# Sums by one-pass products, differences on two engines: a chunk loop of a fused two-layer step

## The chip, the cores and the metric

One core of a Trainium2 chip runs the whole program. The metric is the device time of one execution in microseconds. Engines: TensorE (PE), with its weight loads in rows of their own (PEld), VectorE (DVE), ScalarE (ACT), GpSimd (POOL) and SyncE (SP), which here issues DMAs.

## The reference, cut to what matters

Two layers of a streaming encoder, for 512 prompt and 32 sample positions, f32. Layer 0 mixes by spatial gating and by a Mamba-2 scan. The two parts that the change touches:

```python
s = jnp.einsum('gij,bcjgd->bcigd', w, vc) + b_s[:, :n].T[None, None, :, :, None]   # gMLP, 8 groups, 128 positions
y = u * s
# SSD scan, 16 heads, within a chunk:
cs = jnp.cumsum(dt * a, axis=2)
seg = cs[:, :, :, None] - cs[:, :, None, :]
lmat = jnp.exp(jnp.where(tril, seg, -jnp.inf))
cb = jnp.einsum('bctgn,bcsgn->bctsg', cc, bc)          # 2 groups of 8 heads
y_diag = jnp.einsum('bctsg,bctsgr,bcsgrp->bctgrp', cb, lmat, xs)
# + contribution of the state before the chunk, and the state's update
```

The kernel takes chunks of 128 positions for the scan.

## The kernel before, in words

All activations lie as features on partitions, positions along the free dimension (512 prompt + 32 sample columns). Every dense layer is a row of "slabs" (`slab`, L298): 8 weight tiles of 128x128 against 544 columns, each in three one-pass products (fp32r) of a high and a low part, `w_hi*op_hi + w_hi*op_lo + w_lo*op_hi`, in two column halves of 256 and 288. SP loads the weights into a ring of four, ScalarE makes `w_hi` (L340), POOL `w_lo` (L414), four slabs ahead. All engines have hand-written instruction streams, coupled by counting semaphores; each engine goes through its stream in order.

Around the change:
- `spatial(g)` (L1001), after slabs 4 to 7 of phase `u` and 0 to 3 of `xbc`: per chunk of a group an f32 product that adds the bias (a table of ones times a row padded with zeros) and an f32 product with the spatial weights, into one PSUM bank. VectorE's `ya_out` reads it.
- `cs_sums` (L1017), once, after `spatial(0)`: cumulated sums `cs` and totals, from `da` (positions on partitions). VectorE's `dt_sums` (L1500) copies them out, then `spatial(1)` may run.
- The chunk loop: `chunk(p, rows)` on every engine, five passes: p = 0 the sample (32 rows), p = 1 to 4 the prompt's chunks (128 rows). In each PE turns x, B and C (L1073, L1078) and makes the score table; ScalarE copies them from PSUM (three copies, `x_copied`). Then for four blocks b of four heads `rows_of_cs(b)` (L1083) puts the chunk's sums of each head on all rows, one f32 product per head, in bank 3 (even b) or 2 (odd b); `segments(b)` (L1596, VectorE, L1606) subtracts the own row's sum and takes the minimum with the table `neg` (0 or -3e38), ScalarE's Exp follows, `mixed(b)` (L1610, VectorE, L1616) multiplies by the score table, and `diagonal(b)` (L1096) multiplies with `xs`. Two buffers (`mix`, two halves of 512) serve four blocks. Blocks 2 and 3 need the banks and buffers of 0 and 1 again. After that come the state's part, the state's update and the turn back (L1133).
- `between(n)` (L1053) fills PE's waits: n pieces of the phase `outa`, each an eighth of a slab (six one-pass products). `SSD_PIECES` says how many stand in each of five places. `SSD_MIXED` and `SSD_END` say where the ring's work for finished slabs goes on ScalarE, POOL and VectorE.
- POOL in a pass: `y_skip` (L560, D times x) as soon as the third copy is there, then `xsd` (L566).

```python
rows_of_cs(0); rows_of_cs(1); between(SSD_PIECES[p][0])
rows_of_cs(2); rows_of_cs(3); between(SSD_PIECES[p][1])
diagonal(0); diagonal(1); between(SSD_PIECES[p][2])
diagonal(2); diagonal(3)
```

Of the kernel before, what the change touches and what calls it, by code (L numbers as in the profile page):

```python
# [115 lines left out]
def build(nc, A, O):  # L116
# [27 lines left out]
    with ctx:  # L144
# [30 lines left out]
        neg = sb("neg", P)  # L175
# [255 lines left out]
        SSD_PIECES = ((1, 1, 5, 2, 2),) * NC + ((1, 1, 5, 2, 3),)  # L431
# [5 lines left out]
        N_CONSTS = 7  # L437

# [14 lines left out]
        def _(sp):  # L453
# [37 lines left out]
            for dst, name in ((tri, "tri"), (neg, "neg"), (head_rows, "head_rows"), (conv_state, "conv_state"),  # L491
                              (ffn_state, "ffn_state")):
                load(dst[:, :], A[name])
# [38 lines left out]
        def _(pool):  # L532
# [19 lines left out]

            def chunk(p, rows):
# [10 lines left out]
                if p:  # L564
# [55 lines left out]
        def _(act):  # L620
# [62 lines left out]
            for n in range(KD):  # L683
# [5 lines left out]
                if n == 1:  # L689
# [7 lines left out]
                    run(p_b, p_a, ACT.Exp, "dt_exp", scale=-1.0)  # L697
                if n == 5:
# [42 lines left out]
            def chunk(p, rows):  # L741
# [181 lines left out]
        def _(pe):  # L923
# [77 lines left out]
            def spatial(g):  # L1001
# [15 lines left out]
            def cs_sums():  # L1017
# [3 lines left out]
                mm(Q[:, 2, 128 + NC * SH:128 + NP_], ones[0:TS, :], da[0:TS, NC * SH:NP_]).then_inc(sem("cs_mm"), 1)  # L1021

            for n in range(KD):
# [13 lines left out]
                if n == U_FIRST:  # L1037
                    pe.wait_ge(sem("gm_mask"), 1)
# [834 lines left out]
```

## Time and profile before

| | |
|---|---|
| time, 3 runs | 1857.77 us median (1857.4 to 1858.76) |
| the profiled execution | 1858.24 us, its span 1856.5 us |
| PE busy | 1816.7 us (98%), 14145 matmul records |
| PEld busy | 1768.9 us (95%) |
| DVE, ACT, POOL busy | 955.9 (51%), 622.5 (34%), 847.5 (46%) us |
| mean granted PE clock | 0.991 of full speed |
| chain that ended last | PE 90%, DVE 6%, ACT 2% |

An f32 matmul of the program shows as two records, a one-pass (fp32r) one as a single record. A matmul's length in a row holds its way through the array too: matmuls overlap, so the pace is the distance from start to start. A row of the timeline merges neighbours of one line and form (x16 is 16 records), its length is from the first start to the last end. "[0.19 <- DVE ...]" is idle time of the engine before the row, and what ended it. PEclk is the clock granted to PE, 1.00 for 2.4 GHz and 0.50 for 1.2 GHz.

### The profile page before, as it was taken

Reading aid. Unit: us, or ns where it says so; the run is one execution under the profiler, and the core shown is the slowest. Engines: PE = TensorE matmul, PEld = TensorE weight load, DVE = VectorE, ACT = ScalarE, POOL = GpSimd, SP = SyncE. Lnnn points to the kernel's source line nnn. Section 1 sums busy time; section 2 is a strip of 40 time slices with the busy share of each in tenths; the row PEclk is TensorE's granted clock in tenths of the full one; section 3 lists DMA queues with packets and bytes.
Section 4 is the critical chain, followed back from the end, with each engine's and each line's share of the span. In section 5 each row is a group of like instructions: output and inputs, shape, how many; then the busy total and the mean of one; then the engine's idle time right before and its main releaser. Section 6 shows DMA issues by size and latency. Waiting matters only on the chain.

```text
span 1856.5 us, 34451 instructions
## 1 busy us (share of the span) xinstructions
PE 1816.7 (98%) x14145; PEld 1768.9 (95%) x14145; DVE 955.9 (51%) x1547; ACT 622.5 (34%) x896; POOL 847.5 (46%) x415
## 2 busy tenths in 40 slices
PE   8999999999999999999899999999999999999996
PEld 7999988999999999999899999999899999999995
DVE  6456777565533542556644441344555415515554
ACT  5334423343221222244433332233334313212342
POOL 4333423466544544565533334333365545544662
PEclk9999999999999999999999999999999999999998
DMA  6222201222342232223222222222122222222221
GB/s 231 79 73 69 80 23 35 74 86 80 114 138 89 81 103 90 74 79 98 80 77 77 77 76 80 88 77 78 54 91 82 89 90 90 91 92 82 66 93 48
DMA packets 49475, 156.80 MB, mean 84 GB/s; under 512 B 5984, under 2 KB 10208, under 8 KB 49376
## 3 DMA queue, kind: packets, MB, share of 16 engines
q1 hardware_dynamic: 43776, 147.67, 24.4%
q10 hardware_dynamic: 5600, 7.74, 1.3%
q8 instruction: 71, 1.16, 0.3%
q14 instruction: 28, 0.23, 0.0%
HBM read 149.75 MB, written 5.63 MB: 84 GB/s over the span
## 4 chain that ended last, share of the span: by engine, by line
PE 90%; DVE 6%; ACT 2%; issue 1%; POOL 0%; DMA 0%; DVEq 0%; POOLq 0%; ACTq 0%
PE proj L318 81%; PE Q L925 6%; DVE arena L1753 1%; ACT arena L622 1%; DVE op_lo L389 1%; DVE arena L1616 0%; DVE arena L1606 0%; ACT op_hi L376 0%; PE Q L1202 0%; DVE rstd L369 0%; DVE x L1755 0%; DVE ssq L1426 0%; PE proj L925 0%; DVE arena L1393 0%; PE Q L329 0%
## 5 line engine op out<-in xcount | busy, mean ns | idle before, releaser
L414 POOL TENSOR_TENSOR w_lo<-w_raw,w_hi 128x1024 fp32r<-128x1024 f32 (+2 forms) x276 | 652.3, 2364 | 760.0 <-ACT w_hi L340 759.7
L318 PE MATMUL proj<-op_hi,w_hi 128*128 128x256 f32 (+1 forms) x4272 | 895.6, 291 | 9.5 <-DVE op_lo L389 5.7
L318 PE MATMUL proj<-op_hi,w_lo 128*128 128x256 f32 (+1 forms) x4272 | 884.6, 288 | 0.0
L318 PE MATMUL proj<-op_lo,w_hi 128*128 128x256 f32 (+1 forms) x4272 | 877.8, 287 | 0.0
L318 PEld LDWEIGHTS proj<-op_hi,w_hi 128*128 128x128 f32 x4272 | 683.5, 189 | 22.6 <-issue 12.3
L318 PEld LDWEIGHTS proj<-op_lo,w_hi 128*128 128x128 f32 x4272 | 686.3, 189 | 0.0
L318 PEld LDWEIGHTS proj<-op_hi,w_lo 128*128 128x128 f32 x4272 | 682.0, 188 | 0.0
L340 ACT ACTIVATE w_hi<-w_raw 128x1024 fp32r<-128x1024 f32 (+2 forms) x276 | 284.8, 1032 | 651.0 <-PE proj L318 650.0
L1393 DVE TENSOR_TENSOR arena<-proj,rstd 128x512 f32<-128x512 f32 (+1 forms) x143 | 98.7, 690 | 220.9 <-PE proj L318 195.4
L1400 DVE TENSOR_TENSOR x<-proj,x 128x512 f32<-128x512 f32 x72 | 49.7, 690 | 223.2 <-PE proj L318 223.2
L622 ACT ACTIVATE arena<-arena 128x32 f32<-128x32 f32 (+5 forms) x217 | 106.0, 514 | 54.6 <-DVE arena L1606 33.2
L604 POOL TENSOR_TENSOR arena<-arena,rstd 128x544 f32<-128x544 f32 x44 | 60.0, 1363 | 140.6 <-ACT arena L622 140.6
L405 POOL TENSOR_TENSOR ssq<-ssq,sq 128x544 f32<-128x544 f32 x56 | 90.3, 1613 | 67.7 <-ACT sq L384 67.7
L925 PE MATMUL Q<-arena 128*128 128x256 f32 (+9 forms) x524 | 104.7, 344 | 1.3 <-DVE arena L1616 0.8
L1709 DVE SCALAR_TENSOR_TENSOR arena<-arena,vec 128x546 f32<-128x546 f32 x88 | 96.4, 1095 | 12.4 <-DVE arena L1709 0.3
L925 PEld LDWEIGHTS Q<-arena 128*128 128x128 f32 (+3 forms) x524 | 71.9, 178 | 25.6 <-issue 16.2
L1717 DVE TENSOR_TENSOR arena<-proj,arena 128x512 f32<-128x512 f32 x44 | 30.4, 692 | 120.0 <-POOL arena L604 120.0
L389 DVE SCALAR_TENSOR_TENSOR op_lo<-x,vec,op_hi 128x544 fp32r<-128x544 f32 x48 | 72.1, 1514 | 37.0 <-ACT op_hi L376 33.5
L1707 DVE TENSOR_SCALAR arena<-arena,vec 128x546 f32<-128x546 f32 x44 | 78.2, 1777 | 8.3 <-DVE arena L1697 8.3
L622 ACT ACTIVATE ffn_tail<-arena 128x4 f32 (+1 forms) x44 | 9.1, 206 | 200.0 <-DVE arena L1709 200.0
L1720 DVE TENSOR_TENSOR op_lo<-arena,op_hi 128x544 f32 (+1 forms) x44 | 47.5, 1080 | 40.3 <-ACT op_hi L622 40.3
L622 ACT ACTIVATE op_hi<-arena 128x544 f32 (+2 forms) x46 | 31.0, 678 | 67.5 <-DVE arena L1718 67.5
(171 smaller groups left out, 1040.2 us busy)
## 6 DMA issues: line engine op xcount, KB each, us to landing
w_raw<-in_w_gu SPq DMA_DIRECT2D x88, 512.0 KB, 3.4
w_raw<-in_w_down SPq DMA_DIRECT2D x32, 512.0 KB, 3.4
w_raw<-in_w_heads_a SPq DMA_DIRECT2D x30, 512.0 KB, 3.4
w_raw<-in_w_heads_b SPq DMA_DIRECT2D x18, 512.0 KB, 3.4
w_raw<-in_w_gate SPq DMA_DIRECT2D x16, 512.0 KB, 3.4
w_raw<-in_w_xbc SPq DMA_DIRECT2D x12, 512.0 KB, 3.3
w_raw<-in_w_down SPq DMA_DIRECT2D x16, 384.0 KB, 3.0
w_raw<-in_w_v SPq DMA_DIRECT2D x8, 512.0 KB, 8.2
```

Of the source, the lines that this page charges most:

```text
L318: last = nc.tensor.matmul(proj[:, 2 * g.mod(2) + half, 0:size], w[:, lo:lo + P], o[:, at:at + size], start=(k == 0 and j == 0), stop=(k == ...
L340: nc.scalar.activation(w_hi[:, c:c + width], w_raw[:, c:c + width], ACT.Copy).then_inc(w_hi_done, 1)
L389: nc.vector.scalar_tensor_tensor(out=part(op_lo[ops], n, 0, T), in0=src, scalar=col(gain, n), in1=part(op_hi[ops], n, 0, T), op0=ALU.mult, ...
L405: nc.gpsimd.tensor_tensor(ssq[:, :], ssq[:, :], sq[:, q * T:(q + 1) * T], ALU.add)\
L414: nc.gpsimd.tensor_tensor(w_lo[:, c:c + width], w_raw[:, c:c + width], w_hi[:, c:c + width], ALU.subtract).then_inc(w_lo_done, 1)
L604: nc.gpsimd.tensor_tensor(fsgr[:, q * T:(q + 1) * T], fsg[:, q * T:(q + 1) * T], rstd[:, :], mul).then_inc(sem("f_scaled"), 1)
L622: ins = nc.scalar.activation(dst, src, f, **kw)
L925: return nc.tensor.matmul(out, w, o, start=start, stop=stop)
L1393: a = tt(two(dst(0, TP)), out_prompt(g, rows), two(by[0:rows, f_at:f_at + TP]), mul)
L1400: tt(two(part(x, n, 0, TP)), out_prompt(g), two(part(x, n, 0, TP)), add)
L1707: ins = nc.vector.tensor_scalar(acc, src, w, col(f"fb{layer}", t + -layer * FT), mul, add)
L1709: ins = stt(out=acc, in0=src, scalar=w, in1=acc, op0=mul, op1=add)
```

## The change

- Bias: `bs_pad` holds the bias in rows 0 and 32. ScalarE makes `bias_r` (fp32r) of it, VectorE replaces rows 32 to 63 by the remainder. Each spatial group gets its bias by two one-pass products of 256 columns (two chunks each) and one of 32, where it had four f32 products of 128 and one of 32.
- Sums: `cs_sums` also makes the cumulated sums with heads on partitions (48 rows: three times 16), five more f32 products. ScalarE rounds them into `cs_t` (fp32r), VectorE puts the remainder in rows 32 to 47. `spatial(1)` waits for that.
- POOL's `by_block(p)` spreads a chunk's sums into `cs_b`, four copies each masked by `pick`, so that products with a column of `pick_r` as weights give the rows of four heads. It runs one pass ahead, behind `xsd`; the first one stands before the loop, behind the ring's work for slab `outa` 0.
- `rows_of_cs(b)` is two one-pass products of 256 columns (64 in the sample's pass) in place of four f32 products.
- The differences of blocks 0 and 2 are four Relu on ScalarE (from PSUM, own sum as bias), those of blocks 1 and 3 four tensor_scalar on VectorE. `neg` is gone; the mask is a product of the score table with `tri`, once per pass on VectorE, after `xs`.
- `SSD_PIECES` of the prompt's passes: 1, 2, 4, 2, 2 for 1, 1, 5, 2, 2 (the last with 3).
- The `memset` of `s_prompt` moves from the middle of phase `u` to its end.

The diff, cut:

```diff
+cs_t = nc.alloc_sbuf_tensor_at("cs_t", [P, T], R, offset=ssq_at)
+cs_b = nc.alloc_sbuf_tensor_at("cs_b", [P, 2 * 512], R, offset=sq_at)
+ones_r = nc.alloc_sbuf_tensor_at("ones_r", [P, P], R, offset=w_dt_at)
...
+bias_r = nc.alloc_sbuf_tensor_at("bias_r", [P, D], R, offset=arena_at + 4 * r.at)
 gain_rows = r.take(D)
+da_3 = arena[:, r.at:r.at + 3 * NP_]
...
-SSD_PIECES = ((1, 1, 5, 2, 2),) * NC + ((1, 1, 5, 2, 3),)
+SSD_PIECES = ((1, 1, 5, 2, 2),) + ((1, 2, 4, 2, 2),) * (NC - 1) + ((1, 2, 4, 2, 3),)
...
+def by_block(p, rows):
+
+    c = NC if p == 0 else p - 1
+    if p >= 2:
+        pool.wait_ge(sem("cs_rows"), 4 * (p - 1))
+    out = cs_b[0:HL, (p % 2) * 512:(p % 2) * 512 + 4 * rows].rearrange("p (j t) -> p j t", j=4)
+    nc.gpsimd.tensor_tensor(out, cs_t[0:HL, c * CH:c * CH + rows].unsqueeze(1).broadcast_to([HL, 4, rows]),
+                            pick[0:HL, 0:4].unsqueeze(2).broadcast_to([HL, 4, rows]), mul)\
+        .then_inc(sem("by_block"), 1)
+
+pool.wait_ge(sem("cs_split"), 1)
+pool.wait_ge(consts_in, 16 * N_CONSTS)
+pool.wait_ge(sem("gm_lo"), GROUPS)
+by_block(0, TS)
...
+    if p < NC:
+        by_block(p + 1, CH)
...
+    if n == 0:
+        act.wait_ge(sem("gm_in"), 32)
+        act.wait_ge(sem("v_gained"), GROUPS)
+        run(bias_r[0:64, :], bs_pad[0:64, :], ACT.Copy, "bias_hi")
+        act.wait_ge(sem("wdt_lo"), 1)
+        act.wait_ge(consts_in, 16 * N_CONSTS)
+        run(ones_r[0:64, :], ones[0:64, :], ACT.Copy, "ones_set")
+        run(pick_r[0:HL, :], pick[0:HL, 4:8], ACT.Copy, "ones_set")
+    if n == U_FIRST:
+        act.wait_ge(sem("cs_mm"), 1)
+        act.wait_ge(sem("gm_vn"), GROUPS)
+        run(cs_t[0:HL, 0:TP], Q[0:HL, 3, :], ACT.Copy, "cs_hi")
+        act.wait_ge(sem("cs_copied"), 1)
+        run(cs_t[0:HL, TP:T], Q[0:HL, 2, 256:256 + TS], ACT.Copy, "cs_hi")
...
-        act.wait_ge(sem("seg_done"), 16 * p + 4 * b + 4)
         m = four(mix[0:rows, (b % 2) * 512:(b % 2 + 1) * 512])[:, :, 0:rows]
-        run(m, m, ACT.Exp, "decayed")
+        if b % 2 == 0:
+            act.wait_ge(sem("cs_rows"), 4 * p + b + 1)
+            if p or b:
+                act.wait_ge(sem("y_mm"), 4 * p + b - 1)
+            for j in range(4):
+                h = c * SH + 4 * b + j
+                ins = run(m[:, j, :], Q[0:rows, 3, j * rows:(j + 1) * rows], ACT.Relu,
+                          bias=cs[0:rows, h:h + 1], scale=-1.0)
+            ins.then_inc(sem("gaps_act"), 1)
+            act.wait_ge(sem("gaps_act"), 2 * p + b // 2 + 1)
+            run(m, m, ACT.Exp, "decayed", scale=-1.0)
+        else:
+            act.wait_ge(sem("gaps_dve"), 2 * p + b // 2 + 1)
+            run(m, m, ACT.Exp, "decayed")
...
-    bias = bs_pad[:, g * P:(g + 1) * P]
+    bias = bias_r[0:64, g * P:(g + 1) * P]
     for c in range(NC):
+        if c % 2 == 0:
+            mm(Q[:, q, c * CH:(c + 2) * CH], ones_r[0:64, :], bias.unsqueeze(1).broadcast_to([64, 2, P]),
+               stop=False)
         at = g * VT + c * P
-        mm(Q[:, q, c * CH:(c + 1) * CH], ones[:, :], bias, stop=False)
         mm(Q[:, q, c * CH:(c + 1) * CH], v_tok[:, at:at + P], w_spatial[:, g * P:(g + 1) * P], start=False,
-           stop=True)
-    mm(Q[:, q + 1, 0:TS], ones[:, :], bias[:, 0:TS], stop=False)
+           stop=(c % 2 == 1))
+    mm(Q[:, q + 1, 0:TS], ones_r[0:64, :], bias[:, 0:TS], stop=False)
     mm(Q[:, q + 1, 0:TS], v_tok[:, g * VT + TP:(g + 1) * VT], w_spatial[:, g * P:g * P + TS],
        start=False).then_inc(sem("gm_s"), 1)
...
-    mm(Q[:, 2, 128 + NC * SH:128 + NP_], ones[0:TS, :], da[0:TS, NC * SH:NP_]).then_inc(sem("cs_mm"), 1)
+    mm(Q[:, 2, 128 + NC * SH:128 + NP_], ones[0:TS, :], da[0:TS, NC * SH:NP_])
+    for c in range(NC + 1):
+        rows = CH if c < NC else TS
+        out = Q[0:HL, 3, c * CH:(c + 1) * CH] if c < NC else Q[0:HL, 2, 256:256 + TS]
+        last = mm(out, da_3[0:rows, c * HL:(c + 1) * HL], tri[0:rows, 0:rows])
+    last.then_inc(sem("cs_mm"), 1)
...
     if n == U_FIRST + 1:
-        pe.wait_ge(sem("cs_copied"), 1)
+        pe.wait_ge(sem("cs_split"), 1)
...
             pe.wait_ge(sem("x_copied"), 3 * p + 3)
-        elif b >= 2:
-            pe.wait_ge(sem("seg_done"), 16 * p + 4 * (b - 1))
-        bank = 3 - b % 2
-        for j in range(4):
-            h = hc + 4 * b + j
-            last = mm(Q[0:rows, bank, j * P:j * P + rows], da[0:rows, h:h + 1].broadcast_to([rows, rows]),
-                      tri[0:rows, 0:rows])
+        elif b == 2:
+            pe.wait_ge(sem("gaps_act"), 2 * p + 1)
+        elif b == 3:
+            pe.wait_ge(sem("gaps_dve"), 2 * p + 1)
+        if b == 0:
+            pe.wait_ge(sem("by_block"), p + 1)
+        at = (p % 2) * 512
+        for half in range(2):
+            cols = slice(half * 2 * rows, (half + 1) * 2 * rows)
+            last = mm(Q[0:rows, 3 - b % 2, cols], pick_r[0:HL, b:b + 1].broadcast_to([HL, rows]),
+                      cs_b[0:HL, at + cols.start:at + cols.stop])
         last.then_inc(sem("cs_rows"), 1)
...
-    pe.wait_ge(sem("seg_done"), 16 * p + 16)
+    pe.wait_ge(sem("gaps_act"), 2 * p + 2)
+    pe.wait_ge(sem("gaps_dve"), 2 * p + 2)
...
+    link(nc.vector.tensor_copy(da_3.rearrange("p (c r h) -> p c r h", r=3, h=SH),
+                               by_head(da).unsqueeze(2).broadcast_to([P, NC + 1, 3, SH])))
...
+    lo = slice(2 * SH, HL)
+    dve.wait_ge(sem("cs_hi"), 1)
+    tt(cs_t[lo, 0:TP], Q[lo, 3, :], cs_t[lo, 0:TP], sub)
+    dve.wait_ge(sem("cs_hi"), 2)
+    tt(cs_t[lo, TP:T], Q[lo, 2, 256:256 + TS], cs_t[lo, TP:T], sub).then_inc(sem("cs_split"), 1)
...
+        dve.wait_ge(sem("bias_hi"), 1)
+        tt(bias_r[32:64, :], bs_pad[32:64, :], bias_r[32:64, :], sub).then_inc(sem("bias_lo"), 1)
...
-        nc.vector.memset(s_prompt, 0.0).then_inc(sem("s_zero"), 1)
...
+nc.vector.memset(s_prompt, 0.0).then_inc(sem("s_zero"), 1)
...
+    dve.wait_ge(sem("x_copied"), 3 * p + 3)
+    cb = two(bc_tok[0:rows, 256:512])[:, :, 0:rows]
+    tt(cb, cb, tri[0:rows, 0:rows].unsqueeze(1).broadcast_to([rows, 2, rows]), mul)\
+        .then_inc(sem("cb_masked"), 1)
...
-        if b >= 2:
+        if p or b >= 2:
             dve.wait_ge(sem("y_mm"), 4 * p + b - 1)
-        elif p:
-            dve.wait_ge(sem("y_mm"), 4 * p - 1 + b)
         for j in range(4):
             h = c * SH + 4 * b + j
-            at = (b % 2) * 512 + j * P
-            stt(out=mix[0:rows, at:at + rows], in0=Q[0:rows, 3 - b % 2, j * P:j * P + rows],
-                scalar=cs[0:rows, h:h + 1], in1=neg[0:rows, 0:rows], op0=sub, op1=ALU.min)\
-                .then_inc(sem("seg_done"), 1)
+            at = 512 + j * P
+            ins = nc.vector.tensor_scalar(mix[0:rows, at:at + rows], Q[0:rows, 2, j * rows:(j + 1) * rows],
+                                          cs[0:rows, h:h + 1], 0.0, sub, ALU.min)
+        ins.then_inc(sem("gaps_dve"), 1)
...
-        dve.wait_ge(sem("x_copied"), 3 * p + 3)
+        dve.wait_ge(sem("cb_masked"), p + 1)
...
-    segments(0)
     segments(1)
     mixed(0)
     mixed(1)
-    segments(2)
     segments(3)
...
```

## Rows read from the trace of the kernel before

**Rows 1.** Windows, first pass (two) and third: span, length, busy PE/PEld/DVE/ACT/POOL, PEclk, DMA.

```profile
219.40:226.40 7.00, 4.18 (x51) 3.13 (x50) 4.88 (x13) 4.82 (x11) 4.85 (x2) 1.00 0.32 113
226.40:233.20 6.80, 6.80 (x42) 6.32 (x43) 4.30 (x12) 0.81 (x3) 2.25 (x2) 0.50 0.03 10
266.95:289.24 22.29, 21.98 (x163) 19.46 (x162) 16.52 (x34) 6.80 (x11) 6.55 (x3) 1.00 0.08 24
```

**Rows 2.** Timeline of PE in the third pass: start, length, instruction, idle before.

```profile
268.48 2.01 PE L925 MATMUL Q<-tri,arena 128*128 128x128 f32 x16
270.25 0.50 PE L318 MATMUL proj<-op_hi,w_hi 128*128 128x256 f32 x2
274.15 2.00 PE L925 MATMUL Q<-arena 128*128 128x64 f32 x16 [0.19 <-DVE arena L1616]
```

**Rows 3.** The timelines of VectorE, ScalarE and GpSimd there

```profile
268.70 1.23 DVE L1594 TENSOR_TENSOR arena<-arena 128x1024 f32<-128x1024 f32 x1 [1.77 <-ACT arena L622]
269.84 2.15 DVE L1606 SCALAR_TENSOR_TENSOR arena<-Q,arena,neg 128x128 f32<-128x128 f32 x8
271.91 2.78 DVE L1616 TENSOR_TENSOR arena<-arena 128x512 f32<-128x512 f32 x2
267.58 1.70 ACT L622 ACTIVATE arena<-Q 128x512 f32<-128x512 f32 x3 [1.29 <-PE Q L1073]
269.36 2.33 POOL L560 TENSOR_TENSOR arena<-arena,head_rows 128x1024 f32<-128x1024 f32 x1 [9.69 <-ACT arena L622]
271.65 1.90 POOL L566 TENSOR_TENSOR arena<-arena 128x1024 f32<-128x1024 f32 x1
```

**Rows 4.** The chain of waits there (start, length, what)

```profile
271.91 2.19 DVE arena L1616
```

**Rows 5.** The timeline of PE in the first spatial group

```profile
104.84 0.38 PE L925 MATMUL Q<-arena,ones 128*128 128x128 f32 x2
106.63 0.31 PE L925 MATMUL Q<-arena,ones 128*128 128x32 f32 x2
107.88 0.52 PE L318 MATMUL proj<-op_hi,w_hi 128*128 128x256 f32 x2
108.24 0.41 PE L318 MATMUL proj<-op_lo,w_hi 128*128 128x256 f32 x2
108.49 0.41 PE L318 MATMUL proj<-op_hi,w_lo 128*128 128x256 f32 x2
```

**Rows 6.** The chain of waits at the second spatial group

```profile
114.14 2.24 PE Q L925 x20
```

**Rows 7.** The timelines of VectorE and GpSimd in the u stage

```profile
107.93 2.41 DVE L1512 TENSOR_SCALAR v_tok<-v_tok,ssq 32x128 f32<-32x128 f32 x1
113.67 0.23 DVE L1504 TENSOR_TENSOR arena<-Q,arena 128x80 f32<-128x80 f32 x1
107.54 2.73 POOL L414 TENSOR_TENSOR w_lo<-w_raw,w_hi 128x1024 fp32r<-128x1024 f32 x1 [4.95 <-ACT w_hi L340]
```

**Rows 8.** Groups of ScalarE by form: busy us, mean ns, idle before.

```profile
L622 ACT ACTIVATE arena<-Q 128x128 f32<-128x128 f32 x2 | 0.5, 277 | 11.1 <-PE Q L1133 11.1
```

**Rows 9.** The timelines of PE, VectorE, ScalarE and GpSimd in the first pass

```profile
222.01 0.43 PE L925 MATMUL Q<-tri,arena 32*32 32x32 f32 x8
228.48 1.91 PE L925 MATMUL Q<-arena 32*32 32x64 f32 x16
222.55 2.43 DVE L1594 TENSOR_TENSOR arena<-arena 32x1024 f32<-32x1024 f32 x1 [1.92 <-ACT arena L622]
222.81 1.28 ACT L622 ACT_TABLE_LOAD   x1
221.55 2.36 POOL L414 TENSOR_TENSOR w_lo<-w_raw,w_hi 128x1024 fp32r<-128x1024 f32 x1 [4.14 <-ACT w_hi L340]
```

**Rows 10.** The timeline of PE at two long idles

```profile
903.37 0.82 PE L318 MATMUL proj<-op_hi,w_hi 128*128 128x256 f32 x2 [5.18 <-DVE op_lo L389]
1396.09 0.49 PE L318 MATMUL proj<-op_hi,w_hi 128*128 128x256 f32 x2 [1.39 <-issue]
```

More of the change, by code:

```diff
@@ L161, in build @@
         ARENA = 15200
+        arena_at = nc.sbuf_base
         arena = sb("arena", ARENA)
+        ssq_at = nc.sbuf_base
         ssq = sb("ssq", T)
@@ L174, in build @@
         tri = sb("tri", P)
-        neg = sb("neg", P)
+        sq_at = nc.sbuf_base
         sq = sb("sq", 2 * T)
@@ L184, in build @@
         conv_tail = sb("conv_tail", XBC * 6)
+        w_dt_at = nc.sbuf_base
         w_dt = sb("w_dt", 8 * SH)
@@ L187, in build @@
         w_dt_lo = sb("w_dt_lo", 8 * SH, R)
+        pick = sb("pick", 8)
+        pick_r = sb("pick_r", 4, R)
         rstd_root = sq[:, 0:T]
+        cs_t = nc.alloc_sbuf_tensor_at("cs_t", [P, T], R, offset=ssq_at)
+        cs_b = nc.alloc_sbuf_tensor_at("cs_b", [P, 2 * 512], R, offset=sq_at)
+        ones_r = nc.alloc_sbuf_tensor_at("ones_r", [P, P], R, offset=w_dt_at)
         class Region:
@@ L437, in build @@
         N_CONSTS = 7
+        HL = 3 * SH
         def heads(eng, head, between, drain=None):
@@ L490, in _ @@
             sp.dma_start(gain_rows, A["gain_rows"]).then_inc(sem("gain_in"), 16)
-            for dst, name in ((tri, "tri"), (neg, "neg"), (head_rows, "head_rows"), (conv_state, "conv_state"),
-                              (ffn_state, "ffn_state")):
+            for dst, name in ((tri, "tri"), (head_rows, "head_rows"), (conv_state, "conv_state"),
+                              (ffn_state, "ffn_state"), (pick, "pick")):
                 load(dst[:, :], A[name])
@@ L573, in _ @@
                     low_ahead(pool, PH["outa"], At(n))
+            pool.wait_ge(sem("by_block"), NC + 1)
             pool_squares(pool, "n_yb", "n_in")
@@ L1037, in _ @@
                 if n == U_FIRST:
+                    pe.wait_ge(sem("bias_lo"), 1)
+                    pe.wait_ge(sem("ones_set"), 2)
                     pe.wait_ge(sem("gm_mask"), 1)
@@ L1831 @@
     arrays["tri"] = (t[:, None] <= t[None, :]).astype(f32)
-    arrays["neg"] = np.where(t[:, None] <= t[None, :], 0.0, -3e38).astype(f32)
     kdec = np.exp(lg[None, :] * (CH - 1.0 - t)[:, None])
@@ L1851 @@
     arrays["w_spatial"] = a["gm_w_s"].transpose(2, 0, 1).reshape(P, -1)
-    arrays["bs_pad"] = np.concatenate([a["gm_b_s"].reshape(1, -1), np.zeros((P - 1, D), f32)])
+    arrays["bs_pad"] = np.zeros((P, D), f32)
+    arrays["bs_pad"][0] = arrays["bs_pad"][32] = a["gm_b_s"].reshape(-1)
+    row, four = np.arange(P)[:, None], np.arange(4)[None, :]
+    used = (row < SH) | ((row >= 2 * SH) & (row < 3 * SH))
+    arrays["pick"] = np.concatenate([used & (row % 4 == four), used & (row % SH // 4 == four)], 1).astype(f32)
     arrays["ssm_state"] = a["state_ssm"][0].reshape(SH * SP_, SN).T
```

## The prediction, made before the changed kernel was run

> **What bounds the kernel now.** I read the shares of busy time first: TensorE (PE) works 1816.7 of 1856.5 us, every other engine about half or less, so only work that leaves PE, or waits put in front of it, can move the end. The change touches two stages, so next come the stretches of the chunk loop [rows 1]: in the third of its five passes (266.95 to 289.24) PE is busy 21.98 of 22.29 us at full clock. Then that pass in order of time. PE [rows 2]: four heads' sums are four f32 products of 128 columns; 16 records from 268.48 to 270.25 are eight products, 0.221 us each. An eighth of a slab of `outa` follows (a piece, 0.75 us at the pace below), eight more products, another piece, and the diagonal products at 274.15 after 0.19 us idle for VectorE. So the pass is PE's own work end to end. The other engines [rows 3]: VectorE makes `xs` 268.70 to 269.93, the eight differences of L1606 straight behind it (0.26 us apart), then the products of L1616; ScalarE copies until 269.28; GpSimd (POOL) runs L560 and L566 from 269.36 to 273.55. One thing here decides my forecast: the first L1616 holds the chain for 2.19 us, from 271.91 to 274.09 [rows 4], though the two together take 2.78 [rows 3], which leaves the second about 0.65. It ran only when L566 was done, while L1606, which reads PSUM, passed beside L560 undisturbed.
>
> **Bias.** Per group the spatial stage issues eight f32 products of 128 columns between 104.84 and 106.63, 0.224 us each, then a bias product of 32 columns, 0.31 us with its tail, of which I take 0.14 as its own [rows 5]. Four plus the small one are bias: 4 x 0.224 + 0.14 = 1.04 us. After: two one-pass products of 256 columns. A one-pass pair of 256 + 288 columns takes 0.25 (108.24 to 108.49), so 256 columns take 0.118; the small one at most that. But a one-pass pair behind f32 products takes 0.36 (107.88 to 108.24), 0.11 more, and two of the three now stand behind f32: 0.118 + 0.228 + 0.17 = 0.52. Saved 0.52 a group, 4.2 us in eight. Bounds: 0.3 (each weight change costs more) to 0.85 (no extra), so 2.4 to 6.8. PE stands directly on the path here.
>
> **Sums.** `cs_sums` gets four f32 products of 128 columns and one of 32: 4 x 0.224 + 0.14 = +1.04 us (0.6 to 1.3, as 48 weight columns may load faster). The second spatial group now waits for `cs_split`, not `cs_copied`. The latter came with L1504, over at 113.90, and PE came at 114.14 [rows 6, 7]: 0.24 us of slack. The new chain adds a ScalarE copy, VectorE's two differences (512 and 32 columns) and a hop, about 0.85 us; VectorE comes earlier, for the `memset` of 1024 columns left this stretch and the smaller copy into `da_3` joined it (an estimated 0.55 net). I take 0 and keep up to 0.9. The bias split (some 1 us each on ScalarE and VectorE) ends long before its use at 104.84; the memset falls into a stretch where VectorE waits. The changed constants are one small DMA for another. Nothing for these.
>
> **Rows of sums.** Per prompt pass 16 products of 0.221 (3.54 us) become eight of 0.118 (0.94): 2.6 us less PE work, 10.4 in four passes. With no new wait the loop would give that.
>
> **What the loop waits for instead**, third pass, in the old clock:
> - `rows_of_cs(1)` waits for the third copy, 269.28, behind the first block's products. Those took 0.9 us and hid it; now they take 0.24 from 268.48. PE idles about 0.55. The piece then ends near 270.2.
> - `rows_of_cs(2)` waits for ScalarE's four Relu. Nearest row: a 128x128 copy from PSUM, 277 ns [rows 8]; at 0.2 to 0.28 each they end 270.1 to 270.4. Hidden.
> - `rows_of_cs(3)` waits for `gaps_dve`, VectorE's block 1. Before it in VectorE's queue stands the new mask product on the score table, with two SBUF inputs. L560 has been waiting since 269.36 and starts when `xs` ends, for 1.83 us, to 271.69. That POOL goes first where both wait is shown at 107.54 [rows 7]: its operation took 2.73 us where the same one takes 2.36 [rows 9], so it stood 0.37 behind the VectorE operation of that moment, and the next of VectorE (107.93, all SBUF, a 32x128 piece) took 2.41 and ended just after it. So the mask runs 271.69 to 271.97, the differences to 273.0. PE stands from about 270.3 to 273.05.
> - Two pieces (1.5 us) bring `diagonal(0)` to 274.7. The mask has pushed L566 to 271.97 to 273.85, so `mixed(0)` is 273.85 to 274.4. Behind L566 POOL now has `by_block(p+1)`, half of L566's elements, about 0.95 us (0.6 to 1.3), to 275.35. `mixed(1)` ends at 275.9, and `diagonal(1)`, ready at 275.6, starts 275.95 and is done at 277.05.
> Before, both diagonals ended at 276.15 (2.00 from 274.15) with two pieces behind them; now at 277.05 with three (0.75 more). Net 276.3: 0.15 us later than before, with all 2.6 spent. The later half changes little: Relu and differences of blocks 2 and 3 are done before the four remaining pieces end at 280. Passes two and four, where a weight operation of POOL comes first, come out alike, the last, without `by_block`, 0.4 earlier. Loop: about +0.2 us (bounds -2 to +3 for `by_block` and the mask).
>
> The difference on VectorE is now a tensor_scalar that reads PSUM. L1606 (PSUM) was not held, the tensor_scalar at 107.93 (all SBUF) was [rows 3, 7]; I take the first by its source. Held like the second it would wait behind L566 too, +1.9 us a pass, 7.6 in all.
> The Trainium skill ("SBUF — State Buffer", section "SBUF: two separate sides") says that VectorE and GpSimd share one port pair as an exclusive lock for a whole instruction, on VectorE's side for two SBUF inputs or a two-port mode. By that rule the tensor_scalar from PSUM is free and the mask is held; the trace agrees on the forms it has. By the rule the loop's sum is +0.2, by the nearest row of the same operation +7.8.
>
> **First pass.** `rows_of_cs(0)` ran at 222.01 [rows 9]. It now waits for `by_block(0)`, queued on POOL behind L414 (221.55 to 223.90), and there VectorE's waiting `xs` goes first, to 224.98. So it starts near 225.3; ScalarE's Relu end at 226.3; the table load (1.28), so far done during a wait, can only follow them, so Exp ends at 228.0, `mixed(0)` behind L566 at 229.3, `mixed(1)` behind `by_block(1)` at 230.45. The diagonals, begun at 228.48 and done at 230.4, end near 231.4: +1.0 us (0 to +3, for the clock here).
>
> **The clock.** It is at its low level from 226.4 to 233.2 after seven microseconds in which PE was busy 4.18 [rows 1]. A 5.18 us idle at 898.2 was followed by low clock, one of 1.39 at 1394.7 was not [rows 10]. The new idles are 2.7 to 3.0 us each, with 0.55 and 0.35 beside them: 3.7 of some 7 us, more than the 2.8 before the fall at 226.4, but with denser work around. A fall costs at most half of 6.8 us, 3.4, less what lies in a wait: I take 3.0. I expect two falls in the four prompt passes: +6.0 (0 to +12).
>
> **Sum**, against the profiled execution's own 1858.24 (span 1856.5): -4.2 + 1.04 + 0.2 + 1.0 + 6.0 = +4.0, 1862.3. The median of the runs lies 0.47 lower: 1861.8.
>
> **Rivals.**
> 1. The same waits, no fall of the clock in the four prompt passes. For: the single idle of 1.39 us was not followed by one [rows 10]. Against: the new one is twice that. -4.2 + 1.04 + 0.2 + 1.0 = -2.0: 1855.8.
> 2. The mask product isn't held (VectorE keeps the port from `xs` to the mask). Then the differences end 1.7 us earlier, PE idles 1.0 instead of 2.75, and of 2.6 us a pass about 1.7 stay: -6.8 for the loop, no fall: -4.2 + 1.04 - 6.8 + 1.0 = -9.0: 1848.8. Faster, and it decides wherever the differences end before about 271.5. Against: 107.54 [rows 7].
> 3. All four passes fall (+12) and the first pass stays low longer (+1): 1869. For: the 7 us comparison above.
> 4. The tensor_scalar is held too: another 7.6 on the forecast, 1869.4.
>
> **Chances.** Forecast with one to three falls, 1858.8 to 1864.8: 0.45. Rival 1: 0.18. Rival 2: 0.26. Rivals 3 and 4: 0.11. A change under 0.2% (3.7 us, about what can be told from none) is 1854.1 to 1861.5: it holds most of rival 1 (0.15) and the one-fall end of the forecast (0.15), 0.30. Slower: the rest of the forecast (0.30) and rivals 3 and 4, 0.41. Faster: rival 2, and rival 1 with the bias at its upper bound (0.03), 0.29. Range 1849 to 1869; the forecast's own is 1857 to 1866.
>
> **What would show it.** Spatial groups of about 1.6 us instead of 2.15. In the prompt passes one PE idle of 2.7 to 3 us before the fourth block of sums, released by VectorE's differences, and a mask product of about 2 us that ends just after L560. `mixed(1)` lengthened by `by_block`. In the first pass PE idle over 3 us, released by POOL. PEclk at 0.5 after some of the idles. Wrong if the mask takes 0.3 us or PE's idle stays under 1.2, and wrong in the clock part if PEclk stays at 1.0 through all four.

## The result, and the profile after

The changed kernel takes 1876.22 us (median of 4, 1872.8 to 1877.4) where the kernel before takes 1858.26 on the same chip: ratio 1.0094, 95% interval 1.0081 to 1.0107. It is slower by 18 us. The forecast was 1861.8, the range 1849 to 1869: wrong. The direction had a chance of 0.41.

The profiled execution took 1875.27 us (span 1873.5), 17.0 more than before's 1858.24. PE works 1824.1 us of it, 7 more, though it has 166 fewer matmul records. To find where they are lost, lay the starts of the five passes side by side: the first of the products that turn (transpose) x in each pass. The end is the same product behind the last turn back in each trace. All in us:

| | first turn at | pass 1 | 2 | 3 | 4 | 5 | end |
|---|---|---|---|---|---|---|---|
| before | 220.58 | 23.80 | 22.57 | 22.29 | 23.37 | 23.03 | 335.64 |
| changed | 223.76 | 22.91 | 27.12 | 23.89 | 27.65 | 27.64 | 352.98 |

So 3.2 us are lost ahead of the loop and 14.2 in it; 0.3 are won behind it. First the stretches of the loop in the changed kernel (the columns of [rows 1]; the last row stops 2.1 us short of its pass's end at 352.98):

```profile
223.76:246.68 22.92, 19.21 (x137) 14.77 (x138) 13.31 (x26) 7.68 (x21) 8.63 (x6) 0.93 0.07 24
246.68:273.80 27.12, 24.63 (x139) 21.35 (x137) 17.41 (x28) 8.54 (x18) 10.60 (x5) 0.81 0.12 39
273.80:297.69 23.89, 21.66 (x138) 18.39 (x137) 16.50 (x27) 8.98 (x19) 8.16 (x4) 0.93 0.07 23
297.69:325.34 27.65, 24.37 (x139) 21.09 (x137) 18.34 (x29) 9.04 (x19) 11.04 (x5) 0.81 0.12 39
325.34:350.90 25.56, 23.33 (x128) 20.06 (x127) 14.32 (x24) 7.73 (x17) 6.74 (x3) 0.80 0.07 21
```

Before, the third pass stood at a granted clock of 1.00 [rows 1]; now every pass has a stretch at 0.50 (1.2 GHz). In the trace's record of the clock these low stretches last 3.4, 10.2, 3.4, 10.2 and 10.2 us, one a pass, where before had one of 6.8 in the first.

What TensorE did before each fall, its timeline with the idle ahead of a row in brackets:

```profile
228.46 0.31 PE L980 MATMUL Q<-cs_b,pick_r 48*32 48x64 f32 x4 [3.19 <-POOL cs_b L570]
253.06 0.79 PE L980 MATMUL Q<-cs_b,pick_r 48*128 48x256 f32 x2 [2.12 <-DVE arena L1687]
276.19 0.50 PE L980 MATMUL Q<-cs_b,pick_r 48*128 48x256 f32 x2 [0.26 <-ACT arena L651]
279.91 0.79 PE L980 MATMUL Q<-cs_b,pick_r 48*128 48x256 f32 x2 [1.85 <-DVE arena L1687]
304.86 0.79 PE L980 MATMUL Q<-cs_b,pick_r 48*128 48x256 f32 x2 [2.91 <-DVE arena L1687]
331.45 0.79 PE L980 MATMUL Q<-cs_b,pick_r 48*128 48x256 f32 x2 [1.85 <-DVE arena L1687]
```

The four idles that VectorE's differences (L1687) end are the forecast one, ahead of the fourth block of sums; the low clock begins inside them or as they end (252.62, 279.92, 303.82, 331.12). Before, the only idle among the rows of the third pass was 0.19 us, ahead of the diagonal products [rows 2]. Why L1687 is late stands in the third pass's timelines of VectorE and GpSimd, which answer to [rows 3]:

```profile
275.55 1.23 DVE L1672 TENSOR_TENSOR arena<-arena 128x1024 f32<-128x1024 f32 x1 [1.76 <-ACT arena L651]
276.69 2.13 DVE L1676 TENSOR_TENSOR arena<-arena,tri 128x256 f32<-128x256 f32 x1
278.74 1.11 DVE L1687 TENSOR_SCALAR arena<-Q,arena 128x128 f32<-128x128 f32 x4
279.78 2.79 DVE L1697 TENSOR_TENSOR arena<-arena 128x512 f32<-128x512 f32 x2
276.21 2.33 POOL L586 TENSOR_TENSOR arena<-arena,head_rows 128x1024 f32<-128x1024 f32 x1 [9.69 <-ACT arena L651]
278.50 2.08 POOL L592 TENSOR_TENSOR arena<-arena 128x1024 f32<-128x1024 f32 x1
280.54 1.48 POOL L570 TENSOR_TENSOR cs_b<-cs_t,pick 48x512 fp32r<-48x512 f32 x1
```

The mask product (L1676) lasts 2.13 us and ends at 278.82, 0.28 behind GpSimd's L586 (278.54). Free of GpSimd it takes 0.42 (shown below). A row that is so much longer than the operation itself is called held here. L1687, from PSUM, passes beside L592 at full pace: four in 1.11 us. The two L1697 take 2.79 together, where two free ones take 1.48 (also below). In the chain of waits the mask is now on the path (in place of [rows 4]):

```profile
276.69 2.13 DVE arena L1676
```

Ahead of the loop, the second spatial group in the chain, then its timeline; [rows 6] had 2.24 us, [rows 5] the first group's parts:

```profile
115.24 2.45 PE Q L980 x13
```

```profile
115.17 0.38 PE L980 MATMUL Q<-bias_r,ones_r 64*128 64x256 f32 x1
115.48 0.71 PE L980 MATMUL Q<-arena,v_tok 128*128 128x128 f32 x4
116.12 0.38 PE L980 MATMUL Q<-bias_r,ones_r 64*128 64x256 f32 x1
```

With 13 records instead of 20 the group is longer. From a bias product to the next product pass 0.31 us, where the forecast had 0.12; and from the start of four records of 128 columns (two products, 0.45) to the next bias product 0.64. From the start of one group to the start of the next it is 8.55 us, before 8.24.

### The profile page after: what moved, and what is told of

It reads as the page before. It is cut to its first block, busy times and chain, and to the rows that moved or that the text cites. A ratio compares the mean times of both kernels' runs of the same rounds, so it can differ in the third digit from the quotient of the medians.

```text
span 1873.5 us, 34149 instructions
## 1 busy us (share of the span) xinstructions
PE 1824.1 (97%) x13979; PEld 1767.8 (94%) x13979; DVE 953.8 (51%) x1516; ACT 634.4 (34%) x941; POOL 856.2 (46%) x420
## 4 chain that ended last, share of the span: by engine, by line
PE 85%; DVE 6%; issue 5%; ACT 2%; POOL 2%; DMA 0%; POOLq 0%; DVEq 0%; ACTq 0%
PE proj L328 76%; PE Q L980 6%; POOL w_lo L424 1%; DVE arena L1832 1%; DVE op_lo L399 1%; ACT arena L651 1%; DVE arena L1676 0%; ACT op_hi L386 0%; DVE ssq L1495 0%; PE Q L1271 0%; DVE rstd L379 0%; DVE x L1834 0%; PE proj L980 0%; PE Q L339 0%; DVE arena L1462 0%
## 5 line engine op out<-in xcount | busy, mean ns | idle before, releaser
L424 POOL TENSOR_TENSOR w_lo<-w_raw,w_hi 128x1024 fp32r<-128x1024 f32 (+2 forms) x276 | 654.7, 2372 | 769.0 <-ACT w_hi L350 768.7
L328 PEld LDWEIGHTS proj<-op_hi,w_hi 128*128 128x128 f32 x4272 | 686.2, 189 | 24.5 <-issue 13.3
L980 PE MATMUL Q<-arena 128*128 128x256 f32 (+9 forms) x524 | 108.5, 354 | 1.0 <-DVE arena L1697 0.4
L980 PEld LDWEIGHTS Q<-arena 128*128 128x128 f32 (+3 forms) x524 | 76.2, 189 | 24.5 <-issue 16.2
```

Source lines behind the costliest of these rows:

```text
L328: last = nc.tensor.matmul(proj[:, 2 * g.mod(2) + half, 0:size], w[:, lo:lo + P], o[:, at:at + size], start=(k == 0 and j == 0), stop=(k == ...
L424: nc.gpsimd.tensor_tensor(w_lo[:, c:c + width], w_raw[:, c:c + width], w_hi[:, c:c + width], ALU.subtract).then_inc(w_lo_done, 1)
L980: return nc.tensor.matmul(out, w, o, start=start, stop=stop)
```

## The experiments

Times are medians; beside each stands the ratio to the kernel before on the same chip with its interval. The kernel before gave 1857.9 to 1858.1 throughout.

### Idle filled with products

```diff
                 rows_of_cs(2)
+                for _ in range((0, 16, 14, 22, 14)[p]):
+                    mm(Q[:, 1, 0:256], op_hi[1][:, 0:P], op_hi[1][:, 0:256])
                 rows_of_cs(3)
```

> The changed kernel, with 16, 14, 22 and 14 throwaway one-pass products of 256 columns on TensorE ahead of the fourth block of sums of the four prompt passes (about 0.11 us each, no more than the 1.9 to 2.9 us that TensorE stands idle there); they lengthen no wait. Theory A (the granted clock, which falls after these idles, costs most of the 18 us): the low stretches of 3.4 and 10.2 us go, 12 to 16 us faster than the changed kernel, about 1861 to 1864. Rival B (the waits themselves cost the time, the clock is a by-product): the same idle is only filled, 1875 to 1877.

1863.2 us, 13.0 less than the changed kernel (1.0024, 1.0014 to 1.0033). The windows of the second to fourth pass:

```profile
249.81:272.51 22.70, 22.30 (x154) 18.99 (x153) 17.32 (x28) 8.42 (x18) 10.61 (x5) 1.00 0.15 47
272.51:294.92 22.41, 22.04 (x152) 18.72 (x151) 16.50 (x27) 8.97 (x19) 8.16 (x4) 1.00 0.08 24
294.92:318.33 23.41, 22.95 (x160) 19.64 (x159) 18.32 (x28) 9.03 (x19) 11.03 (x5) 1.00 0.14 46
```

The products do nothing useful and shorten no wait: in the second pass the fourth block of sums starts 6.39 us behind the pass's start, in the changed kernel 6.38. Yet the four prompt passes take 91.6 us instead of 106.3: with the idle filled the clock stays at 2.4 GHz, and that is worth 14.7 us. What is left is what the kernel before takes there (91.3): the waits have eaten the saving of 2.6 us a pass and no more. The first pass, left as it was, had a low stretch of 13.7 us this time (26.0 us against 22.9), which takes 3.1 back. It does the same work after the same idle of 3.19 us in both, so the idle alone does not set how long the clock stays low.

### Bias products over 128 rows

```diff
-                bias = bias_r[0:64, g * P:(g + 1) * P]
+                bias = bias_r[:, g * P:(g + 1) * P]
```
(and `ones_r[:, :]` in both products; rows 64 to 127 of the bias are zero)

> The changed kernel, with the bias products of the spatial groups over 128 contraction rows (rows 64 to 127 hold zeros) instead of 64. Theory C (TensorE pays some 0.2 to 0.3 us each time it goes between a product over 64 rows and one over 128): a group falls from 2.45 us to 1.7 to 1.9, eight groups, 4 to 6 us faster than the changed kernel, about 1871. Rival D (going between one-pass and f32 products is what costs, whatever their rows): a group stays at 2.4, 1876.

1867.64 us, 8.6 less (1.0050, 1.0033 to 1.0067). The chain's row and the group's timeline:

```profile
115.17 1.65 PE Q L980 x13
```

```profile
115.17 0.38 PE L980 MATMUL Q<-bias_r,ones_r 128*128 128x256 f32 x1 [0.65 <-DVE cs_t L1580]
115.39 0.61 PE L980 MATMUL Q<-arena,v_tok 128*128 128x128 f32 x4
115.75 0.36 PE L980 MATMUL Q<-bias_r,ones_r 128*128 128x256 f32 x1
115.95 0.61 PE L980 MATMUL Q<-arena,v_tok 128*128 128x128 f32 x4
```

The same products over twice the rows are faster: group to group 7.46 us instead of 8.55. Call it a going when TensorE goes from a product over 128 rows to one over 64, or back. The three bias products of a group mean six goings, 1.09 / 6 = 0.18 us each.

### f32 bias products over 64 rows in the kernel before

```diff
-                bias = bs_pad[:, g * P:(g + 1) * P]
+                bias = bs_pad[0:64, g * P:(g + 1) * P]
```
(and `ones[0:64, :]`)

> The kernel before, with its f32 bias products of the spatial groups over 64 contraction rows instead of 128 (the left-out rows hold zeros); no one-pass product anywhere in them. Theory C, on its own: each of the five bias products of a group, which stand between products over 128 rows, costs some 0.3 us more, 1.5 us a group, eight groups: 8 to 13 us slower than before, 1866 to 1871. Rival D (rows cost nothing, one-pass beside f32 does): 1858.

1873.59 us, 15.7 slower than before (1.0088, 1.0071 to 1.0105), above the expected 8 to 13.

```profile
115.30 4.01 PE Q L925 x20
```

```profile
115.23 0.48 PE L925 MATMUL Q<-arena,ones 64*128 64x128 f32 x2
115.64 0.49 PE L925 MATMUL Q<-arena,v_tok 128*128 128x128 f32 x2
116.06 0.48 PE L925 MATMUL Q<-arena,ones 64*128 64x128 f32 x2
```

Group to group 10.08 instead of 8.24: 1.84 us for ten goings, 0.18 each again, with no one-pass product in it. So the change of rows is what costs, not one-pass beside f32. The expectation was low for two reasons: a bias product costs 0.37 us more (in and out), not 0.3, which makes 14.7 us in eight groups; and the first pass is 1.1 us longer (24.92 against 23.80), with a low stretch of 10.2 us instead of 6.8. The Trainium skill ("TensorEngine Tiling (Array Packing)", section "Key Properties") says that "Changing tiling mode (not just tile) drains the TensorE"; its section "Tiling Modes" lists 64 rows as a mode of their own. A drain at each going would fit the 0.18 us, but no trace here shows the mode or the drain; the price is from the traces.

### The bias part alone, over 128 rows, in the kernel before

The diff is the change's bias part with the two lines above.

> The kernel before, with the change's bias part alone, and its one-pass bias products over all 128 contraction rows (rows 64 to 127 hold zeros). Theory C (the going between 64 and 128 rows ate the gain of the bias part): a spatial group takes 1.65 us as in the run with 128 rows instead of 2.15 to 2.2, eight of them, 4 us faster than before, about 1854. Rival D (the bias part has no gain of its own, what the run with 128 rows won lay in the changed kernel's other parts): 1858.

1854.17 us (0.9977, 0.9967 to 0.9986): 3.9 faster than before, as expected. Over all 128 rows, the bias part alone is a gain of about the forecast size, though not by the forecast's sum: a group saves 0.78 us (8.24 to 7.46), 6.2 in eight; a new wait of 1.61 us for VectorE's `dt_sums` ahead of the second group and a first pass that is 1.1 longer (24.88 against 23.80, low stretch 10.2 us) take most of the difference back.

### Sums products over 128 rows

```diff
+            nc.gpsimd.tensor_scalar(cs_b[:, :], w_spatial[:, 0:1024], 0.0, None, mul)
-     pick_r[0:HL, b:b + 1].broadcast_to([HL, rows]), cs_b[0:HL, ...]
+     pick_r[:, b:b + 1].broadcast_to([P, rows]), cs_b[:, ...]
```

> The changed kernel, with the one-pass products of the sums over 128 contraction rows (rows 48 to 127 hold zeros, set once by GpSimd ahead of the loop) instead of 48. Theory C: about 0.3 us less of TensorE for each of four blocks of a pass; what of it is on the path is the first and the second block and what stands behind the third, 0.3 to 1.0 us a pass, 2 to 5 us in all. Rival D: nothing, 1876.

1868.69 us, 7.5 less (1.0065, 1.0048 to 1.0082), more than either theory gave. PE's idle ahead of the fourth block is not shorter (10.1 us in four passes, 8.7 in the changed kernel), but each low stretch of the prompt passes lasts 3.4 us where three lasted 10.2: passes of 24.0, 23.8, 24.7 and 24.5. What the rows do for the work itself is seen further down, where no idle disturbs it.

### The mask product behind the differences

```diff
+                segments(1)
                 dve.wait_ge(sem("x_copied"), 3 * p + 3)
                 tt(cb, cb, tri...)      # the mask product
-                segments(1)
                 mixed(0)
```

> The changed kernel, with VectorE's mask product behind the differences of the second block instead of ahead of them; nothing else is moved. Theory E (the mask is held until GpSimd's product ends, and it alone makes the fourth block of sums wait): the idle of 1.9 to 2.9 us there goes, the mask is held further behind by GpSimd's next product instead, the third and fourth head block's chain is 1 to 2 us earlier and fewer clock falls stay: 1862 to 1870. Rival F (the idle only goes to the first diagonal product, which waits for the masked table through the same chain, and the clock falls there): 1874 to 1877.

1865.94 us, 10.3 less (1.0040, 1.0027 to 1.0053). The idle ahead of the fourth block goes in three of the four prompt passes; in the second the diagonals wait instead, 1.12 and 0.34 us, for products held in their turn. VectorE there:

```profile
253.00 1.09 DVE L1697 TENSOR_TENSOR arena<-arena,tri 128x256 f32<-128x256 f32 x1
254.19 3.65 DVE L1692 TENSOR_TENSOR arena<-arena 128x512 f32<-128x512 f32 x2
```

In the fourth pass a shorter idle stays ahead of the fourth block, and the clock is low from 302.86 for 10.2 us (the pass takes 26.4):

```profile
301.91 0.50 PE L980 MATMUL Q<-cs_b,pick_r 48*128 48x256 f32 x2 [0.85 <-DVE arena L1682]
```

### GpSimd's products behind the second masked-decay product

```diff
                 pool.wait_ge(sem("x_copied"), 3 * p + 3)
+                pool.wait_ge(sem("mixed"), 4 * p + 2)
```

> The changed kernel, with GpSimd's three products of a pass (skip term, xsd, next sums table) let go only once VectorE has done its second masked-decay product of that pass. Theory E (VectorE and GpSimd hold one another off, and so the mask, the two products and with them the fourth block of sums come late): the mask takes 0.4 us instead of 2.1, the next two products 0.7 each, TensorE no longer stands idle ahead of the fourth block, the falls of the granted clock go with the idle; four passes of 27.1, 23.9, 27.6 and 25.3 us come to 22 to 23 each, 12 to 17 us faster than the changed kernel, 1859 to 1864. Rival G (it is ScalarE's four-step differences and the chain through them that is late): the idle stays, 1874 to 1877; or the three products come so late that the end of the pass waits for them, 1876 and more.

1858.96 us, 17.3 less (1.0000, 0.9990 to 1.0009): as much as the whole loss, with one wait. The ten runs lie between 1854.4 and 1860.1. VectorE in the third pass, then the passes' windows:

```profile
272.89 0.42 DVE L1677 TENSOR_TENSOR arena<-arena,tri 128x256 f32<-128x256 f32 x1
273.23 1.12 DVE L1688 TENSOR_SCALAR arena<-Q,arena 128x128 f32<-128x128 f32 x4
274.27 1.48 DVE L1698 TENSOR_TENSOR arena<-arena 128x512 f32<-128x512 f32 x2
```

```profile
249.03:270.00 20.97, 20.20 (x139) 17.01 (x137) 14.87 (x28) 8.42 (x18) 9.96 (x5) 1.00 0.15 51
270.00:290.66 20.66, 20.14 (x138) 16.95 (x137) 14.07 (x27) 8.97 (x19) 7.80 (x4) 1.00 0.09 26
```

The mask takes 0.42 us (2.13 when held). Of the 2.6 us of PE work saved in a pass, 1.6 now show (22.57 to 20.97, 22.29 to 20.66).

### The first sums table early

```diff
+            by_block(0, TS)
             low_ahead(pool, PH["outa"], At(0))
-            by_block(0, TS)
```

> The changed kernel, with GpSimd's first sums table ahead of its low split of the second outa slab instead of behind it. Theory H (TensorE's 3.2 us idle in the first pass is this product's queueing behind the split): that idle goes and the first pass is 2 to 3 us shorter, unless the clock falls otherwise: 1873 to 1875. Rival: the split comes 1.4 us later and the first piece of outa waits for it, 1876.

1877.02 us (1.0092, 1.0076 to 1.0109): no gain. The 3.2 us idle released by GpSimd is gone, and one of 3.3 us stands ahead of the fourth block of the same pass, since VectorE's mask is now held beside GpSimd's L586 (227.06 to 229.94):

```profile
225.75 2.43 DVE L1672 TENSOR_TENSOR arena<-arena 32x1024 f32<-32x1024 f32 x1 [1.95 <-ACT arena L651]
228.11 1.91 DVE L1676 TENSOR_TENSOR arena<-arena,tri 32x64 f32<-32x64 f32 x1
```

```profile
230.71 0.32 PE L980 MATMUL Q<-cs_b,pick_r 48*32 48x64 f32 x2 [3.30 <-DVE arena L1687]
```

The idle had a second cause behind the first. Both come from VectorE and GpSimd holding one another: in the changed kernel the first table stands behind L424 and VectorE's `xs`, here the mask behind L586.

### All four, and three of them

The first run has the 128 rows of both kinds, GpSimd's wait and the early table; the other leaves the sums products at 48 rows.

> The changed kernel with all of these: bias products and sums products over 128 rows, GpSimd's three products after the second masked-decay product, the first sums table early. If the causes are separate, the parts add up: 9 us of the bias rows, 13 to 16 of GpSimd's order with the clock, 2 to 3 of the first table, 1 to 4 of the sums' rows: 1844 to 1851, faster than both kernels. If they share one cause (the clock falls alone), no more than the best of them and the bias: 1855 or more.

> The changed kernel with bias products over 128 rows, GpSimd's order and the first table early, but the sums products over 48 rows as in the change. The run with 128 rows in both took 1846.0. Theory C applied to the sums: undisturbed passes of 20.7 to 21.0 us instead of 20.5 to 20.8, 1846.5 to 1848. If the rows of the sums matter as much by themselves as the run that changed them alone suggests (7.5 us): 1850 or more.

1846.02 us (0.9933, 0.9916 to 0.9949) and 1848.78 us (0.9951, 0.9935 to 0.9968). The causes are separate and nearly add up: alone the four were worth 8.6, 7.5, 17.3 and -0.8 us, 32.6 in sum, together 30.2. The first kernel is 12 us faster than before. In passes without a low stretch the rows of the sums are worth 0.1 to 0.2 us (20.92 and 20.66 against 20.78 and 20.47); of the 2.1 us between the two profiled executions, 1.6 lie in the fourth pass (23.22 against 21.58), where the 48-row kernel had a low stretch and the other none. So most of the 7.5 us of the sums' rows was probably clock too; no run tells why their number shortens the low stretches.

### The gain without the change's loop

The kernel before with the bias part over 128 rows and GpSimd's wait.

> The kernel before, with the bias part over 128 rows and with GpSimd's two products of a pass let go only after VectorE's second masked-decay product: it holds what can be had without the change's loop. If GpSimd's order is the whole gain and the loop's new sums give none: the same as the changed kernel with the four corrections, 1846. If the new sums are worth what the undisturbed passes show (20.5 us against 22.3): 1850 to 1854.

1852.22 us (0.9969, 0.9956 to 0.9981). GpSimd's order is worth 0.5 us a pass there (22.10, 21.86, 22.86). What is left to 1846, 6.2 us, comes with the changed loop: the new sums and what was moved around them. No run parts these further.

### A piece into the remaining idle

With all four, TensorE still stood idle for 1.8, 0.8, 0.5 and 1.5 us ahead of the fourth block, in the first four passes. The pieces of `outa` become 2, 1, 4 in place of 1, 2, 4 (1, 1, 5 in the first pass), and the mask goes behind the differences.

> The last version of the changed kernel (128 rows, GpSimd's order, first table early), with the mask product behind the differences of the second block and one outa piece moved from behind the third and fourth block of sums to ahead of the third: it lies where TensorE still stands idle for 1.8, 0.8, 0.5 and 1.5 us. If the piece fills these idles and the first pass's clock fall goes with them: 3 to 6 us off 1846, 1840 to 1843. If the diagonal products then wait for the masked table instead: 1844 to 1847.

1850.43 us (0.9958, 0.9941 to 0.9975), 4.4 more than without: missed. The first pass came to 19.4 us, but the second and third take 25.4 and 24.1. VectorE, and then GpSimd, in the second:

```profile
244.69 5.59 DVE L1695 TENSOR_TENSOR arena<-arena 128x512 f32<-128x512 f32 x2
```

```profile
245.94 1.48 POOL L571 TENSOR_TENSOR cs_b<-cs_t,pick 48x512 fp32r<-48x512 f32 x1
247.39 2.33 POOL L424 TENSOR_TENSOR w_lo<-w_raw,w_hi 128x1024 fp32r<-128x1024 f32 x1
```

The second of the two L1695 by itself, and TensorE behind it:

```profile
246.45 3.82 DVE L1695 TENSOR_TENSOR arena<-arena 128x512 f32<-128x512 f32 x1
250.33 0.90 PE L983 MATMUL Q<-arena 128*128 128x64 f32 x3 [2.64 <-DVE arena L1695]
```

It is the fourth masked-decay product of its pass and stands in the trace from 246.45 to 250.27: beside L571, and let through only behind L424, which followed at once. TensorE waited 2.64 us for it, and the clock fell (low from 249.38 for 6.8 us).

### The next table behind the fourth masked-decay product

```diff
+                pool.wait_ge(sem("mixed"), 4 * p + 4)
                 if p < NC:
                     by_block(p + 1, CH)
```

> The version with the pieces moved, and GpSimd's next sums table (and with it the low split behind it) only behind VectorE's fourth masked-decay product of the pass. Theory E (the hold by two GpSimd products in a row is what TensorE waited for): the fourth product takes 0.7 us instead of 3.8, the waits of 2.6 us and the clock falls behind them go, passes of 19.4 us and four of about 20: 1837 to 1842. Rival (the pieces ahead of the third block make the third differences late, whatever GpSimd does): waits of 1 us or more stay there, 1846 to 1850.

> The same, with the mask product at its first place, ahead of the differences of the second block. With GpSimd silent there it takes 0.4 us, and the moved piece covers it: the same time as the other run of this pair within 1 us if its place no longer matters, 1837 to 1843; 2 us or more above it if the place matters by itself.

1839.70 us (0.9902, 0.9886 to 0.9919) and 1839.64 us (0.9900, 0.9883 to 0.9916): the best version, 18 us faster than before and 36 faster than the change, and the place of the mask no longer matters. The two L1696 of the second pass, which took 5.59 us (as L1695) without the new wait, now take 2.44:

```profile
244.57 2.44 DVE L1696 TENSOR_TENSOR arena<-arena 128x512 f32<-128x512 f32 x2
```

The first three prompt passes of the same run, with none below full clock:

```profile
235.95:256.05 20.10, 19.54 (x139) 16.80 (x137) 15.24 (x28) 8.42 (x18) 9.26 (x5) 1.00 0.17 53
256.05:275.88 19.83, 19.26 (x139) 16.75 (x137) 14.36 (x27) 8.98 (x19) 7.10 (x4) 1.00 0.09 28
275.88:296.75 20.87, 19.80 (x139) 16.84 (x137) 16.19 (x28) 9.04 (x19) 9.47 (x5) 1.00 0.16 51
```

22.29 us in the third pass [rows 1] have become 19.83, 2.5 less: about the 2.6 us of products saved, though GpSimd's order gave 0.4 to 0.5 of it in the kernel before too.

## Why the prediction was wrong, step by step

The forecast for the profiled execution was 1862.3, it took 1875.27. Two steps were wrong by more than that together, 15.4 us; smaller errors took some back.

- **Bias: wrong, in sign.** Forecast -0.52 us a group, measured +0.31 (8.24 to 8.55), for eight groups +2.5 instead of -4.2: 6.7 us. The working priced columns and a change between f32 and one-pass at 0.11, from rows in which every product had 128 rows, and allowed nothing beyond that: "each weight change costs more" was its lower bound, +0.3 saved. It passed over that the new products have 64, and put the going between the two at nothing. Two runs show 0.18 us for each going, in one-pass (six a group) and in f32 (ten a group). With 128 rows a group saves 0.78, inside the bounds of 0.3 to 0.85. The sign named for it, groups of about 1.6 us, came only there (1.65); the changed kernel's took 2.45.
- **The clock: right in mechanism, wrong in size.** Forecast two falls of at most half of 6.8 us in the prompt passes, +6.0; there were four, and three of them had low stretches of 10.2 us, 34.1 in all. Filling the idle gives 14.7 us back: 8.7 more than forecast. Rival 3 had the four falls (+12), but shared a chance of 0.11 with rival 4; rival 1, no fall, is out. The price of a fall was taken from the one low stretch in the loop before.
- **Mask held, differences not: right.** Forecast a mask of about 2 us that ends just behind GpSimd's skip product (L560, now L586), differences unheld, an idle of 2.7 to 3.0 us; measured 2.13 us of mask, 1.11 for the four differences, idles of 2.12, 1.85, 2.91, 1.85. The fourth block of the third pass came 4.48 us behind the first one (275.43 to 279.91), forecast 4.57; the idle in front of it was shorter than forecast because TensorE's own work was longer, 1.37 us from the second block to the third (276.19 to 277.56) against 0.24 + 0.75. `mixed(1)` was lengthened by `by_block` as forecast: it is the second L1697 and ends 0.55 us behind L570. Rivals 2 and 4 (whose 1869.4 lay just outside the stated range) fall with this. The runs with GpSimd's wait show the hold by taking it away.
- **The loop without the clock: right.** Forecast +0.2 us in all; with the idle filled the four passes took 91.6 against 91.3.
- **The wait for the third copy: right.** From the first block's start to the second's 0.24 + 0.55 = 0.79 us forecast, 0.76 measured (275.43 to 276.19).
- **Sums:** forecast +1.04; the first group with `cs_sums` to the second is 1.49 longer, of which 0.31 is the bias, so +1.2. No wait for `cs_split` appeared; it does once the groups are short (0.65 us in the run with bias products over 128 rows).
- **First pass:** the idle of over 3 us released by GpSimd came (3.19), but the pass is 0.9 shorter, not 1.0 longer. Its low stretch was 3.4 us instead of 6.8; in the run with the early table, and in the filled one, it was 6.8 and 13.7 and the pass 24.8 and 26.0. What sets the length of a low stretch is open.

Summed: 6.7 for the bias, 8.7 for the clock, 0.2 for the sums, 0.1 for the loop, -1.9 for the first pass, 13.8. No term was forecast for the 0.3 us won ahead of the first group, which starts at 104.54 instead of 104.84, nor for the 0.3 behind the loop; with them it is about the 13.0 missed. The -1.9 of the first pass is luck, not insight: the same pass took 26.0 us in the filled kernel, where the clock stayed low for longer.

What stays open: why low stretches lasted 3.4 us in some passes and 10.2 in others after like idles (1.85 us both in the third and in the fifth). The profiled executions show only that they are shorter with the sums over 128 rows, and absent from the prompt passes of the version with all four and of the best one.

## What to carry to other kernels

Before a product is made shorter, look at its rows: one over part of the rows between products over all of them can cost more than it saves, and zeros in the rest of the rows cost TensorE nothing here. When VectorE and GpSimd both work from SBUF near the critical path, decide by a wait which goes first; here one wait on GpSimd turned a loss of 1% into none, and two waits, with the rows filled up, the first table early and a piece moved, into a gain of 1%. An idle of 2 us of TensorE in dense work has to be priced with the clock behind it, which cost 14.7 us here, while the waits themselves took about the 10.4 us that the new sums saved.

## What the runs showed of the hardware beyond that

- Going between products over 64 and over 128 rows cost TensorE 0.18 us each way, in f32 and in one-pass products (1.84 us for ten goings, 1.09 for six).
- Two GpSimd products in a row held one VectorE product of 0.69 us for 3.82 us: it did not get in between them. In the changed kernel's third pass the mask, waiting behind L586, did get in ahead of L592 (it ends at 278.82, L592 at 280.58); what decides is not shown. VectorE's differences that read PSUM ran beside the same kind of product unhindered, 0.28 us each.
- Idles of 1.85 us were followed by a fall to 1.2 GHz. In the fourth pass one of 1.19 us was, in the run with GpSimd's wait (296.11; low from 296.50 for 3.4 us), and one of 0.85 us, in the run with the mask behind the differences (301.91; low from 302.86 for 10.2 us). In the same pass one of 1.54 us was not, in the version with all four, nor was one of 0.81 us in the kernel before (294.35). So the length of the last idle alone does not tell whether the clock falls. Throwaway products in the place of the idle, and nothing else, kept 2.4 GHz.
